# Expert layers of a hybrid trunk: exponentials among the gelus, one-hot columns in a ring of 32 tokens, the spread copied out for eight tokens at a time

## The reference, cut to what matters

```python
q = _f(xt @ w_q).reshape(n, PK_HEADS, 2, PK_HALF)
s = jnp.einsum('thcd,hcnd->thcn', q, _f(keys))
sv, si = lax.top_k(s, PK_TOPK)
cand = (sv[:, :, 0, :, None] + sv[:, :, 1, None, :]).reshape(n, PK_HEADS, PK_TOPK * PK_TOPK)
best, bi = lax.top_k(cand, PK_TOPK)
i1 = jnp.take_along_axis(si[:, :, 0], bi // PK_TOPK, axis=-1)
i2 = jnp.take_along_axis(si[:, :, 1], bi % PK_TOPK, axis=-1)
...
gate = jax.nn.softmax(best, axis=-1)
...
act = jax.nn.gelu(_f(jnp.einsum('td,ted->te', xi, u_tab[ei]))) * gi
return jnp.einsum('te,ted->td', act.astype(xi.dtype), v_tab[ei])
```

## Time and profile before

| what | value |
|---|---|
| median of 3 runs | 4829.74 us (4828.92 to 4830.86) |
| profiled execution, its own time | 4826.63 us |
| its span in the profile | 4824.8 us |
| PE busy | 4345.4 us, 90% |
| DVE busy | 2959.8 us, 61% |
| POOL busy | 1612.7 us, 33% |
| ACT busy | 777.9 us, 16% |
| mean granted TensorE clock | 0.95 |

### The profile page before, as it was taken

How to read it: one execution, slowest core, us unless ns; L and a number is a source line. 1 busy time by engine, 2 the same in 40 slices (tenths; PEclk the granted TensorE clock), 3 DMA queues, 4 the chain that set the end, 5 groups by cost and what they waited for, 6 DMA issues and landing times. The chain is left out here.

```text
span 4824.8 us, 44699 instructions
## 1 busy us (share of the span) xinstructions
PE 4345.4 (90%) x15514; PEld 2533.4 (53%) x15514; DVE 2959.8 (61%) x5907; ACT 777.9 (16%) x1630; POOL 1612.7 (33%) x1472
## 2 busy tenths in 40 slices
PE   6799557987999999999979988698889999999997
PEld 2464343756555455545536866365665545555453
DVE  4444882787975666647634226379797656654763
ACT  1210451116300000000012223110640000000000
POOL 0000510006665555546400000000666655554640
PEclk8899778999999999999989988799999999999999
DMA  3120442115799899979911101121579989998992
GB/s 142 53 89 0 176 176 109 49 66 158 270 358 383 329 388 351 367 291 405 354 70 63 65 25 9 66 83 58 156 259 357 390 324 386 353 362 304 390 360 99
DMA packets 354146, 1048.48 MB, mean 217 GB/s; under 512 B 31641, under 2 KB 132361, under 8 KB 342234
## 3 DMA queue, kind: packets, MB, share of 16 engines
q0 software_dynamic: 148128, 545.35, 29.7%
q1 hardware_dynamic: 106748, 450.27, 24.7%
q10 hardware_dynamic: 99072, 50.33, 3.7%
HBM read 991.70 MB, written 54.14 MB: 217 GB/s over the span
## 5 line engine op out<-in xcount | busy, mean ns | idle before, releaser
L580 PE MATMUL banks<-h_dense_T,blocks 128*128 128x384 f32 x4096 | 1362.9, 487 | 35.1 <-ACT dense_act L459 35.1
L615 PE MATMUL banks<-blocks,picked_T 128*128 128x512 f32 x3072 | 1359.3, 594 | 16.0 <-DVE picked_T L797 16.0
L580 PEld LDWEIGHTS banks<-h_dense_T,blocks 128*128 128x128 f32 x4096 | 779.9, 191 | 624.9 <-issue 144.1
L615 PEld LDWEIGHTS banks<-blocks,picked_T 128*128 128x128 f32 x3072 | 585.2, 191 | 708.8 <-issue 652.1
L424 POOL DMA_INDIRECT expert_rows<-in_pk_u_dram,expert x512 | 667.9, 1305 | 488.5 <-DVE own_dots L812 279.3
L424 POOL DMA_INDIRECT expert_rows<-in_pk_v_dram,expert x512 | 603.8, 1179 | 537.9 <-DVE acc L831 255.0
L831 DVE SCALAR_TENSOR_TENSOR acc<-expert_rows,expert_weight,acc 128x1024 f32<-128x1024 f32 x504 | 624.3, 1283 | 83.5 <-DMA expert_rows<-in_pk_v_dram,expert 82.7
L812 DVE CUSTOM_DVE_ANT_0 expert_rows<-expert_rows,h_rows 128x1024 f32<-128x1024 f32 x512 | 598.8, 1221 | 33.2 <-DMA expert_rows<-in_pk_u_dram,expert 32.8
L797 DVE TENSOR_TENSOR picked_T<-dense_act,shared 128x384 f32<-128x384 f32 x256 | 218.7, 855 | 627.1 <-PE banks L615 627.0
L459 ACT ACTIVATE dense_act<-banks 128x384 f32<-128x384 f32 x256 | 125.3, 490 | 2291.5 <-PE banks L580 2291.5
L415 POOL TENSOR_SCALAR shared<-iota,picked_T 128x128 f32<-128x128 f32 x192 | 118.4, 630 | 571.1 <-ACT picked_T L465 505.6
(11 more groups left out here) (445 smaller groups left out, 4442.0 us busy)
## 6 DMA issues: line engine op xcount, KB each, us to landing
blocks<-in_pk_u_turned_dram SPq DMA_DIRECT2D x256, 512.0 KB, 6.7
blocks<-in_pk_v_dram SPq DMA_DIRECT2D x256, 512.0 KB, 6.7
gates_dram<-shared ACTq DMA_DIRECT2D x48, 1024.0 KB, 5.1
shared<-gates_dram SPq DMA_DIRECT2D x32, 1536.0 KB, 11.3
ada_block<-in_ada_rest_dram SPq DMA_DIRECT2D x32, 1280.0 KB, 7.6
blocks<-in_pk_w_q_dram SPq DMA_DIRECT2D x32, 512.0 KB, 3.3
MIXT<-in_ev_w_in_dram SPq DMA_DIRECT2D x16, 512.0 KB, 3.6
expert_rows<-in_pk_u_dram,expert POOLq DMA_INDIRECT x512, 8.3
```

What stands on the lines that cost most here:

```text
L580: mm = pe.matmul(dense_dots(c), u[:, k * P:(k + 1) * P], HT[:, k, :], start=(k == 0), stop=(k == KD - 1))
L615: mm = pe.matmul(ps[:, at_:at_ + HALF], wt[:, c % WEIGHED, z * P:(z + 1) * P], v[:, half_ * HALF:(half_ + 1) * HALF], start=(c == 0), stop ...
```

## The change

1. `exponentials(0)` stands behind the gelu of chunk 5 in ScalarE's list, where it stood ahead of the gelu of chunk 0.
2. The ring of one-hot columns is 32 tokens, in `expert_rows` (the buffers for the idle rows' transfers, not in use then), where it was 16 tokens in `shared` and `acc`. ScalarE makes its first columns four to five groups ahead of the copy (`HOTS_AHEAD`), where it was two.
3. The copy out of the spread takes eight tokens (two banks, 1024 columns) in one instruction, and TensorE has six PSUM banks in three pairs for it, where it had four single ones. Banks 4 and 5 are those from which the columns are copied, so TensorE waits for all three `cols_out` ahead of the spread.

```diff
-HOTS = 16
+HOTS = 32
+HOTS_AHEAD = 4
...
-        first_hot = [h.rearrange("p (b n) -> p b n", n=P)
-                     for h in (shared[:, 4 * D:5 * D], acc[:, 0, :])]
-        second_hot = [h.rearrange("p (b n) -> p b n", n=P)
-                      for h in (shared[:, 5 * D:6 * D], acc[:, 1, :])]
+        first_hot, second_hot = (rows[:, 4 * b:4 * b + 4, :].rearrange(
+            "p b (t n) -> p (b t) n", n=P) for b in range(2))
...
             def spread_tile(z):
-                for g in range(z * P // 4, (z + 1) * P // 4):
-                    if g + 2 < DENSE // 4 and by_act(g + 2):
-                        first_hots(g + 2)
-                    k, part = g // (BATCH // 4), g % (BATCH // 4)
+                for q in range(z * P // 8, (z + 1) * P // 8):
+                    for g in range(2 * q + HOTS_AHEAD, 2 * q + HOTS_AHEAD + 2):
+                        if g < DENSE // 4 and by_act(g):
+                            first_hots(g)
+                    k, part = q // 2, q % 2
                     if part == 0 and k >= 2:
                         act.wait_ge(gates_put[k % 2], 16 * (k // 2))
-                    act.wait_ge(spread, 4 * (g + 1))
-                    at_ = (g % 4) * HALF
-                    act.activation(staged[k % 2][:, :, 4 * part:4 * part + 4, :],
-                                   ps[:, at_:at_ + HALF].rearrange("p (t g j) -> p g t j", t=4,
-                                                                   j=KEYS_A_GROUP),
+                    act.wait_ge(spread, 8 * (q + 1))
+                    at_ = 2 * (q % 3) * HALF
+                    act.activation(staged[k % 2][:, :, 8 * part:8 * part + 8, :],
+                                   ps[:, at_:at_ + 2 * HALF].rearrange(
+                                       "p (t g j) -> p g t j", t=8, j=KEYS_A_GROUP),
                                    ACT.Copy).then_inc(spread_out, 1)
...
             for z in range(ND):
-                exponentials(z)
+                if z:
+                    exponentials(z)
                 for c in range(EARLY[z], EARLY[z + 1]):
+                    if c == 6:
+                        exponentials(0)
                     gelu(c)
                 columns(z)
...
             def spread_tile(z):
                 for g in range(z * P // 4, (z + 1) * P // 4):
-                    if g >= 4:
-                        pe.wait_ge(spread_out, g - 3)
+                    if g % 2 == 0 and g >= 6:
+                        pe.wait_ge(spread_out, g // 2 - 2)
...
             pe.wait_ge(dots_out, EARLY[ND])
+            pe.wait_ge(cols_out, ND)
             for z in range(ND):
                 spread_tile(z)
```

More of the change, by code:

```diff
@@ L352, in hot @@
         def hot(hots, n, count=1):
-            at_ = n % (HOTS // 2)
-            two = hots[n // (HOTS // 2) % 2]
-            return two[:, at_, :] if count == 1 else two[:, at_:at_ + count, :]
+            at_ = n % HOTS
+            return hots[:, at_, :] if count == 1 else hots[:, at_:at_ + count, :]
         def dense_dots(c):
@@ L482, in spread_tile @@
             def spread_tile(z):
-                for g in range(z * P // 4, (z + 1) * P // 4):
-                    if g + 2 < DENSE // 4 and by_act(g + 2):
-                        first_hots(g + 2)
-                    k, part = g // (BATCH // 4), g % (BATCH // 4)
+                for q in range(z * P // 8, (z + 1) * P // 8):
[3 more added lines that the diff above has]
+                    k, part = q // 2, q % 2
                     if part == 0 and k >= 2:
                         act.wait_ge(gates_put[k % 2], 16 * (k // 2))
-                    act.wait_ge(spread, 4 * (g + 1))
-                    at_ = (g % 4) * HALF
-                    act.activation(staged[k % 2][:, :, 4 * part:4 * part + 4, :],
-                                   ps[:, at_:at_ + HALF].rearrange("p (t g j) -> p g t j", t=4,
-                                                                   j=KEYS_A_GROUP),
+                    act.wait_ge(spread, 8 * (q + 1))
[3 more added lines that the diff above has]
+                                       "p (t g j) -> p g t j", t=8, j=KEYS_A_GROUP),
                                    ACT.Copy).then_inc(spread_out, 1)
-                    if part == BATCH // 4 - 1:
-                        act.wait_ge(spread_out, g + 1)
+                    if part == 1:
+                        act.wait_ge(spread_out, q + 1)
                         act.dma_start(gates[:, :, k * BATCH:(k + 1) * BATCH, :].rearrange(
@@ L516, in _ @@
             act.wait_ge(iota_done, 2)
-            for g in range(2):
+            for g in range(HOTS_AHEAD):
                 if by_act(g):
@@ L604, in spread_tile @@
                     for j in range(4):
-                        n, at_ = 4 * g + j, (g % 4) * HALF + j * P
+                        n, at_ = 4 * g + j, (g % 6) * HALF + j * P
                         pe.matmul(ps[:, at_:at_ + P], hot(second_hot, n), hot(first_hot, n),
```

## The result

The changed kernel takes 4756.91 us (median of 4 runs, 4755.15 to 4758.66), against 4829.33 for the kernel before in the same comparison: a ratio of 0.9847, with a 95% interval of 0.9833 to 0.9862. That is 72.4 us less. The forecast was 4771.3 with a range from 4759 to 4788.

What follows compares the result with a forecast made beforehand. Late exponentials held up TensorE in step 2; in the spread three engines were taken for 91 to 93%, losing some 10 us handing over. Terms 19.4 + 18.2 + 11.5 + 9.3 = 58.4 us gave 4771.3, range 4759 to 4788.

Steps and rivals of the forecast that it cites:

- The exponential: Step 2: with exponential 0 behind gelu 5, TensorE runs without a break; 19.4 and 18.2 us gained in the two layers.
- The wait for the columns' copy: Ahead of the spread: TensorE's new wait for the third `cols_out` is on the path, 0.5 us in each layer.
- The spread: Ring and copy: the stage takes 121.5 us, set by ScalarE, gaining 11.5 us in layer 0 and 9.3 in layer 1.
- that saves 48 x 0.03 = 1.4 of the 121.0: Spread, ScalarE: taken for 121.0 us (109.0 busy plus 24 x 0.5); wide copies at 1.03 us, against 1.06 a pair, save 1.4.
- the landing of transfers: Spread, ScalarE: a transfer lands 5.4 us after its issue, so waits for it add 6 x 0.3 = 2 us.
- The bounds of POOL and VectorE: Spread, counted from its start S: POOL's work ends at S + 118.5, VectorE's at S + 114.4.
- The slow stretches of layer 0: Layer 0's spread took 4.3 us more, with the clock at 0.83 in one stretch; half was taken as gained.
- That the ring wasn't the cost: Rival: the spread stays as long as it is, only 37.6 us are gained, 4792; 14 in 100.
- The bare work: Rival: the spread reaches 118 us and layer 0 loses its slow stretches, 4762; 6 in 100 beyond 4759.

Runs made afterwards that it cites:

- e7: Changed kernel with TensorE's wait for the three column copies moved from the spread's start to its third pair of banks; 4756.36 us (0.9843).
- e3: Changed kernel with single banks and copies of four tokens again, ring of 32 and early first columns kept; 4768.16 us (0.9877).
- e12: Changed kernel with three staging buffers for ScalarE's transfers instead of two; 4764.34 us (0.9859).
- e1: Kernel before with only the move of exponential 0 behind gelu 5; 4793.64 us (0.9924).
- e2: Changed kernel with exponential 0 back in its old place, ring of 32 and copies of eight tokens kept; 4797.23 us (0.9942).
- e4: Changed kernel with a ring of 16 tokens and first columns two groups ahead, wide copies and six banks kept; 4792.86 us (0.9931).
- e10: Changed kernel with three of ScalarE's 30 groups of first columns a layer given to POOL, ring left at 32 tokens; 4778.10 us (0.9887).

## Why the prediction was wrong, point by point

**The exponential.** The mechanism and each of its steps held. The third chunk follows the second without a gap, exponential 0 ends at 1041.3, or 33.3 us after chunk 0, where 33.1 was forecast (1043.8 - 1010.7), and VectorE waits for none. The terms were 19.4 and 18.2 us, the stages measured 19.8 in both layers. In layer 1 the first two chunks were slow in the kernel before too, 11.49 us and not 10.49, which the sum left out. The fall of the clock went with the gap: in the stretch that answers to the earlier trace rows, TensorE was busy for all 5 us, with a granted clock of 1.00 (2.4 GHz):

```profile
1035.00:1040.00 5.00, 5.00 (x17) 2.94 (x16) 4.90 (x5) 0.84 (x2) 0.00 (x0) 1.00 0.28 99
```

**The wait for the columns' copy.** It was put at 0.5 us a layer on the path. It delays the first product by 0.43, but not the end (e7): group 1 needs a column from ScalarE, which has the same copy ahead of it.

**The spread: this step failed.** The prediction took 121.5 us; measured are 116.2 and 117.4, so 11.5 of the 13 us by which the sum fell short of the span's change are here (18.9 and 13.4 against 11.5 and 9.3; 2.1 of the 11.5 belong to the slow stretches below). The mechanism was right: a deeper ring and wider copies let the busiest engines work with few waits. The size of the bound was not. ScalarE was named as the last engine, and ended the second spread; POOL ended the first. The step is "that saves 48 x 0.03 = 1.4 of the 121.0", and the 121.0 itself:

- ScalarE's 109.0 us of busy time weren't all work. An instruction that follows at once starts some 0.1 us before the one ahead ends, and one that has waited does not. e3 has the same instructions as the kernel before, and ScalarE is busy for 104.65 and 103.97 of its stages. These windows leave out the copies that fall behind the stage, and not the same number in each. Counted from the spread's start to the end of its last copy, with all 96 copies and all 30 groups of columns, it is 109.6 us before and 105.9 us in e3, in both layers, though the durations of the single instructions add up to the same (125.0 and 125.4). So 3.7 us of the 109.0 were overlaps lost at waits, and came back.
- The copy took 1.006 us in the median, and a copy of half the width 0.589, so a pair saves 0.17 and not 0.03 where the two stand apart. From e3 to the changed kernel the busy time, counted in this way, falls by 3 us (105.9 to 102.9 and 102.8), where 1.4 was taken. The VectorE page of the Trainium skill (The TRN2 errata) gives ScalarE 172 cycles and one for each column out of PSUM at 1.2 GHz. An estimate by that page is 0.997 us for 1024 columns and 0.570 for 512, so 0.14 saved a pair. The traces' 1.006 and 0.589 agree within 0.02 us.
- For the landing of transfers 2 us were added. The changed kernel has three such waits in each spread, 2.2 and 3.7 us, with an issue in each. e12, which is without them, has ScalarE's last first column 2.1 and 3.6 us earlier, so this term was about right.
- What is left between 109.0 and the changed kernel's 101.73 and 100.86, 0.6 and 1.3 us, is work that falls behind the end of the stage: ScalarE's last copy ends 1.2 and 2.1 us after it.

With 101.73 + 24 x 0.5 = 113.7, ScalarE is taken for 98% of the first spread.

**The bounds of POOL and VectorE.** POOL was put at S + 118.5; it ran 112.07 us for 44 groups where 114.0 was taken, 0.637 us a column and not 0.648; the rows of before held many short bursts, those of the changed kernel one. With a start at S + 3.1 and the last group its bound is S + 116.2, and that is the length of the first spread. VectorE was put at S + 114.4 with TensorE's last group in it; its last column ended at S + 112.0, so the like figure is S + 113.1. Both were too high, by 2.3 and 1.3 us, as ScalarE was. Why a column of POOL's takes a little less isn't shown.

**The slow stretches of layer 0.** I took half of the 4.3 us back; all came. e1 has them again with the ring of 16 (134.77, clock 0.97), in e2 and in the changed kernel they are gone. e4, with the ring of 16 too, has them in both layers (0.94). e10, with the ring of 32, has them again (0.97 and 0.96). In the kernel before they are two stretches of 3.4 us with a granted clock of 0.50, at 1148.6 and 1193.0, each within 1 us of the end of a pause of TensorE's of over 2 us. TensorE's waits in the two spreads before, longest one last:

```profile
PE banks L606 <- issue: 34.2, 37, 2.2
PE banks L606 <- issue: 32.3, 39, 1.5
```

The idle time is nearly the same in both layers, but its longest piece is 2.2 us in layer 0 and 1.5 in layer 1. In before, e1, e4 and e10 together the clock fell 13 times, 12 times within 1.4 us of the end of a pause of 1.9 to 2.4 us and once behind one of 1.2; seven of e4's 17 pauses of that length brought none. The changed kernel's longest pauses are 1.4 and 1.8 us. So the falls go with the longer pauses, more isn't shown, and why layer 0 before had them and layer 1 not stays open.

**The rivals.** That the ring wasn't the cost is refuted by e4. The bare work, with 6 in 100 beyond 4759, was nearest to what came, and it should have had more: all three engines were sized by busy times of the kernel before, and all three came out too high. For ScalarE it is shown that its busy time held something which the change removes.

**The rest.** 2.7 us came ahead of chunk 0, 3.2 were lost later, and the medians are 1.0 us further apart than the spans: none of it can be put down to the change, as far as these runs show.

## What to carry to other kernels

Where several engines are each taken for over nine tenths of a stage and meet in a ring, a deeper ring can take away most of what they lose by waiting for each other, as here; size each engine by instructions times their distance in a row that has no waits, not by its busy time, which falls with the waits. One engine's uninterrupted stretch doesn't prove that it is the only bound: giving POOL room moved 1 us, until work was taken from ScalarE as well. Reading when each engine's last piece is done, in every run, tells which one ended the stage. Where an engine's list begins with an instruction whose input comes late (an exponential ahead of gelus), look at the order of the list first: that move alone gave 39 of the 72 us.

## What the runs showed of the hardware that was not expected

- ScalarE's busy time for the same 96 copies and 30 groups of columns was 109.6 us in the kernel before and 105.9 in e3, where more of them follow each other at once; such an instruction starts 0.1 us before the one ahead ends.
- The short ring with wide copies (e4) took 132.6 and 132.9 us with a granted clock of 0.94 in the mean, where the deep ring has 1.00: 12 of the 13 falls seen in the spreads came within 1.4 us of the end of a pause of TensorE's of 1.9 to 2.4 us, though not every such pause brought one.
- Giving 12 more columns a layer to an engine that was level cost 9.7 us (e10): 6.6 by the columns, and most of the other 3.1 because the last 32 products ran with a granted clock of 0.50, after a pause of 2.37 us.
